# Even layer: input slabs in another order, scan levels among them, the spatial bias on VectorE, output products begun by operand halves

## The reference, cut to what matters

```python
z = h @ w_in
a_u, a_v, b_q, b_f, b_i, b_g = jnp.split(z, [...], axis=-1)      # 512 columns each
a_u, a_v = gelu(a_u), gelu(a_v)
# spatial half: chunks of 128 tokens, 8 heads of 64
v = rms_norm_2(a_v, v_norm)
mixed = einsum('hts,bcshd->bcthd', tril(w_s), v) + b_s.T
a_out = a_u * mixed
# scan half: 4 heads of 128, a gated linear recurrence
f = lb + (1 - lb) * sigmoid(b_f);  k = 1 - f
o_t = q_t . state_t,  state_t = diag(f_t) state_(t-1) + k_t v_t^T   # q = b_q, v = b_i
o = rms_norm_2(o, out_norm) * silu(b_g)
m = concatenate([a_out, o]) @ w_out
```

## Time and profile before

| | |
|---|---|
| median of 3 runs | 1850.38 us (1849.93 to 1851.93) |
| profiled execution | 1851.3 us, its span 1849.3 us |
| TensorE busy | 1744.8 us, 94% |
| VectorE, ScalarE, POOL busy | 1247.6, 878.9, 38.8 us |
| even layer, second input slab to ffn_1 | 912 to 1059 us |

### The profile page before, as it was taken

The page is one execution under the profiler, slowest core; times in us unless marked ns, Lnnn a source line. Parts: engine busy times, 40 slices in busy tenths (PEclk is TensorE's granted clock), DMA queues, the critical chain, the costliest instruction groups (busy, mean ns, idle before and its releaser), DMA issues.

```text
span 1849.3 us, 32552 instructions
## 1 busy us (share of the span) xinstructions
PE 1744.8 (94%) x13634; PEld 1623.0 (88%) x13634; DVE 1247.6 (67%) x1305; ACT 878.9 (48%) x916; POOL 38.8 (2%) x39
## 2 busy tenths in 40 slices
PE   7998997799899999999997899998999999899997
PEld 7987896799899998999995799997999997899997
DVE  5676654774588888666776576667766686576666
ACT  5365332453434436444653454456544462554445
POOL 0000000000000000000003000000000000000000
PEclk9999998899899999999997999998999997899999
DMA  7523334254244453554550245443455441245541
GB/s 282 184 93 114 144 126 156 95 201 161 92 160 190 157 197 137 188 192 166 208 183 36 74 165 202 181 179 140 159 191 194 164 173 51 87 170 192 192 166 63
DMA packets 42646, 286.91 MB, mean 155 GB/s; under 512 B 4704, under 2 KB 6880, under 8 KB 9152
## 3 DMA queue, kind: packets, MB, share of 16 engines
q1 hardware_dynamic: 38528, 273.70, 40.8%
q0 software_dynamic: 2800, 10.69, 1.6%
q10 hardware_dynamic: 1232, 1.25, 0.2%
HBM read 281.42 MB, written 4.19 MB: 154 GB/s over the span
## 4 chain that ended last, share of the span: by engine, by line
PE 84%; DVE 10%; ACT 3%; issue 2%; DMA 1%; POOL 0%; DVEq 0%; ACTq 0%; POOLq 0%
PE PS L367 83%; DVE arena L1664 3%; DVE ring_lo L1661 2%; ACT arena L1132 1%; DVE arena L1661 1%; ACT ring_hi L1132 1%; DMA arena<-in_mem_t 1%; ACT L1132 0%; DVE inv L1718 0%; DMA ring_raw<-in_w_stream 0%; DVE operand L1724 0%; PE PS L706 0%; DVE arena L1797 0%; DVE arena L1792 0%; DVE inv L2383 0%
## 5 line engine op out<-in xcount | busy, mean ns | idle before, releaser
L367 PE MATMUL PS<-operand,ring_hi 128*128 128x256 f32 (+1 forms) x4776 | 1127.2, 321 | 33.2 <-DVE operand L1724 21.5
L367 PEld LDWEIGHTS PS<-operand,ring_hi 128*128 128x128 f32 x4776 | 799.5, 193 | 104.5 <-issue 18.3
L367 PE MATMUL PS<-operand,ring_lo 128*128 128x256 f32 x3092 | 877.2, 284 | 0.0
L1661 DVE TENSOR_TENSOR ring_lo<-ring_raw,ring_hi 128x2048 fp32r<-128x2048 f32 x260 | 599.2, 2308 | 220.0 <-ACT ring_hi L1132 219.7
L1132 ACT ACTIVATE ring_hi<-ring_raw 128x2048 fp32r<-128x2048 f32 x260 | 494.7, 1908 | 226.5 <-PE PS L367 221.4
L367 PEld LDWEIGHTS PS<-operand,ring_lo 128*128 128x128 f32 x3092 | 594.9, 192 | 0.1
L367 PE MATMUL PS<-hidden_hi,ring_hi 128*128 128x256 f32 x880 | 249.0, 283 | 1.3 <-DVE hidden_lo L1661 1.3
L367 PE MATMUL PS<-hidden_lo,ring_hi 128*128 128x256 f32 x880 | 249.0, 283 | 0.0
L367 PE MATMUL PS<-hidden_hi,ring_lo 128*128 128x256 f32 x880 | 248.9, 283 | 0.0
L1132 ACT ACTIVATE arena<-PS 128x512 f32<-128x512 f32 (+4 forms) x123 | 79.7, 660 | 327.2 <-PE PS L367 312.1
L367 PE MATMUL PS<-arena 64*64 64x64 f32 (+7 forms) x2200 | 159.5, 264 | 25.6 <-DVE arena L1664 13.1
(11 more groups left out here) (145 smaller groups left out, 964.5 us busy)
## 6 DMA issues: line engine op xcount, KB each, us to landing
ring_raw<-in_w_stream SPq DMA_DIRECT2D x260, 1024.0 KB, 4.8
spilled_gates<-arena POOLq DMA_DIRECT2D x12, 256.0 KB, 2.3
arena<-spilled_gates POOLq DMA_DIRECT2D x2, 1536.0 KB, 9.3
tables<-in_tables POOLq DMA_DIRECT2D x1, 1344.0 KB, 10.8
residual<-in_x_t ACTq DMA_DIRECT2D x4, 256.0 KB, 6.1
arena<-in_mem_t POOLq DMA_DIRECT2D x1, 1024.0 KB, 13.2
out_t<-residual SPq DMA_DIRECT2D x4, 256.0 KB, 2.1
arena<-in_spatial_t POOLq DMA_DIRECT2D x1, 512.0 KB, 3.7
```

The lines of the kernel that those rows point to most:

```text
L367: return nc.tensor.matmul(out, lhs, rhs, start=start, stop=stop, skip_group_check=True)
L1661: return v.tensor_tensor(out, a, b, op)
```

## The change

The order of the input slabs becomes f, q, v, u, i, g (`EVEN_ORDER`, applied by SP when it issues the DMAs). TensorE does level 0 and 1 of the scan behind the fifth slab and one level behind most slabs after it; spatial mixing stands behind the ninth. Levels 1 to 7 multiply only the later halves of the columns, 64 of 128, into one bank. The bias of spatial mixing leaves TensorE: VectorE multiplies by the gain, now a column of each partition, and adds the bias, which a DMA has laid on 128 partitions, in four fused operations. ScalarE takes exp(-x) of the early and exp(x) of the late half instead of Abs and Exp of everything, takes values v and i out of PSUM itself, and squares v. The first three output slabs run by halves: tiles 0 to 3 of all three, then tiles 4 to 7 of all three, in three banks. The diff, cut to its core:

```diff
+EVEN_ORDER = [4, 5, 2, 3, 8, 9, 0, 1, 10, 11, 6, 7]
...
-        spatial_w = AM = area(14, 8, P)
-        v_gain = area(15, 1, W)
+        spatial_w, AM = area(14, 8, P), area(13.5, 8, HD)
+        spatial_b, v_gain = area(15, 4, P), small[:, 58:62]
+        av_squares, mixed = area(2, 4), area(2, 4)
...
+            stream_turns(3, even // 3 - 1)
+            for n, at in enumerate(EVEN_ORDER):
+                sp.wait_ge(lo_split, even + n - 2)
+                sp.dma_start(ring_raw[:, n % 3, :], stream[even + at]).then_inc(landed[n % 3], 16)
+            turns_ = (N_SLABS - rest) // 3
+            stream_turns(rest, turns_)
...
-            pool.dma_start(spatial_b, ins["spatial_b"]).then_inc(sem("spatial_landed"), 16)
-            pool.dma_start(v_gain[:, 0, :], ins["v_gain"].to_broadcast([P, W])).then_inc(sem("spatial_landed"), 16)
+            for q in range(2):
+                pool.dma_start(spatial_b[rows_of(q)], ins["spatial_b"].rearrange("o (f q s) -> q o f s", f=4, q=2)[q]
+                               .to_broadcast([HD, 4, P])).then_inc(sem("spatial_landed"), 16)
+            pool.dma_start(v_gain, ins["v_gain"].rearrange("o (f p) -> p (o f)", p=P), allow_slow_non_contiguous=True).then_inc(sem("spatial_landed"), 16)
             pool.wait_ge(sem("gl_factors"), 1)
-            pool.wait_ge(sem("spatial_ready"), 1)
             for li in range(1, 9):
...
-            project("even_in", 0, 8, fresh=EVERY, norm=True, by_token=True)
-            project_by_token("even_v", 0, 4)
...
-                        mm(o, AV[:, tt, h * HD:(h + 1) * HD], spatial_w[:, h, :], True, False)
-                        last = mm(o, table("ones")[0:1, 0:HD], spatial_b[:, h * P:(h + 1) * P], False, True)
-            last.then_inc(sem("spatial_mixed"), 1)
...
+            def level(li):
                 pe.wait_ge(sem("gl_factors"), li + 1)
                 if li >= 2:
                     pe.wait_ge(sem("gl_added"), li - 1)
-                if li < 8:
+                if li == 0:
                     for tt in range(2):
-                        tok = slice(tt * P, (tt + 1) * P)
                         for h in range(4):
-                            k = KB[:, h, tok] if li == 0 else XM[li % 2][:, h, tok]
-                            q = BQ[:, h, tok] if li == 0 else XM[li % 2][:, h, tok]
-                            last = mm(bank(2 + 2 * (li % 2) + tt)[:, h * P:(h + 1) * P], k, q)
+                            tok = slice(tt * P, (tt + 1) * P)
+                            last_ = mm(bank(5 + tt)[:, h * P:(h + 1) * P], KB[:, h, tok], BQ[:, h, tok])
+                elif li < 8:
+                    later = halves(XM[li % 2], LEVELS[li - 1])[1]
+                    n = T // (4 * LEVELS[li - 1])
+                    for tt in range(2):
+                        for h in range(4):
+                            o = bank(3 + li % 2)[:, (4 * tt + h) * HD:(4 * tt + h + 1) * HD]
+                            last_ = mm(o.rearrange("p (n c) -> p n c", n=n), XM[li % 2][:, h, tt * P:(tt + 1) * P],
+                                       later[:, h, tt * n:(tt + 1) * n, :])
                 else:
                     for h in range(4):
-                        last = mm(bank(2)[:, h * P:(h + 1) * P], XM[0][:, h, 0:P], XM[0][:, h, P:T])
-                last.then_inc(sem("gl_pairs"), 1)
-            pe.wait_ge(sem("gl_added"), 9)
-            for h in range(4):
-                o, c = bank(6 + h // 2)[:, h % 2 * T:(h % 2 + 1) * T], slice(h * P, (h + 1) * P)
-                mm(o[:, 0:P], BI[:, 0, c], AT[:, h, :])
-                mm(o[:, P:T], BI[:, 1, c], AT[:, 4 + h, :], True, False)
-                last = mm(o[:, P:T], BI[:, 0, c], AC[:, h, :], False, True)
-                if h % 2:
-                    last.then_inc(sem("gl_out"), 1)
-            for h in range(2):
-                pe.wait_ge(sem("gl_squares"), h + 1)
-                mm(bank(2 + h), table("ones"), flat(KB)[:, 512 * h:512 * (h + 1)]).then_inc(sem("gl_norms"), 1)
+                        last_ = mm(bank(3)[:, h * P:(h + 1) * P], XM[0][:, h, 0:P], XM[0][:, h, P:T])
+                last_.then_inc(sem("gl_pairs"), 1)
...
+            def spatial():
+                pe.wait_ge(sem("spatial_ready"), 1)
+                pe.wait_ge(sem("gl_added"), 1)
+                for f in range(4):
+                    for tt in range(2):
+                        for q in range(2):
+                            h = 2 * f + q
+                            last_ = mm(bank(5 + f // 2)[rows_of(q), f % 2 * T + tt * P:f % 2 * T + (tt + 1) * P],
+                                       AV[:, tt, h * HD:(h + 1) * HD], spatial_w[:, h, :])
+                last_.then_inc(sem("spatial_mixed"), 1)
...
+            def even_out(j, first, last_=None):
+                slot, _, g = place(START["even_out"] + j)
+                pe.wait_ge(lo_split, g + 1)
+                for m in range(2):
+                    for k in range(first, first + KT // 2):
+                        last_ = block_product(bank((7, 3, 4)[j])[:, m * T:(m + 1) * T], slot, m * KT + k,
+                                              XH[:, 8 + k, :], XL[:, 8 + k, :], k == 0 and m == 0, k == KT - 1)
+                return last_
+            by_dve, by_act = sem("even_taken"), sem("even_values")
+            even_slab(0, None, fresh=EVERY)
+            even_slab(1, None, between=lambda: norm_sum(True))
+            even_slab(2, None)
+            even_slab(3, (by_dve, 1))
+            even_slab(4, (by_dve, 2), True)
+            pe.wait_ge(by_dve, 4)
+            level(0)
+            level(1)
+            even_slab(5, (by_dve, 3), True)
+            level(2)
+            even_slab(6, (by_dve, 4))
+            level(3)
+            even_slab(7, (by_act, 1))
+            level(4)
+            even_slab(8, (by_act, 2), True)
+            pe.wait_ge(sem("spatial_landed"), 64)
+            spatial()
+            level(5)
+            even_slab(9, (by_dve, 5), True)
+            level(6)
+            even_slab(10, (by_dve, 6), between=lambda: level(7))
+            level(8)
+            scan_out()
+            even_slab(11, (by_act, 3), between=scan_norms)
             operands(1)
-            residual_project("even_out", 8, (4, 6))
+            for j in range(3):
+                even_out(j, 0)
+            operands(2)
+            for j in range(3):
+                even_out(j, KT // 2).then_inc(multiplied, 1)
+            output_slab(START["even_out"] + 3, 8, bank(5))
...
+            def gl_exp(li):
+                act.wait_ge(sem("gl_diff"), li)
+                early, late = halves(DIF[li % 2], LEVELS[li - 1] if li < 8 else P)
+                run(early, early, ACT.Exp, scale=-1.0)
+                run(late, late, ACT.Exp).then_inc(sem("gl_exp"), 1)
...
-                d = flat(DIF[li % 2])
-                step(run(d, d, ACT.Abs))
-                run(d, d, ACT.Exp, scale=-1.0).then_inc(sem("gl_exp"), 1)
...
+            split_slab(even + 12)
+            values(9, BI[:, :, T:2 * T], ACT.Copy)
+            split_slab(even + 13)
...
+            split_slab(even + 14)
             step(last)
             for h in range(2):
                 run(roots[h], roots[h], ACT.Exp, scale=-0.5).then_inc(sem("gl_root"), 1)
+            even_act(7, BG, ACT.Silu)
...
-            dve.wait_ge(sem("spatial_mixed"), 1)
-            mul(flat(AU), flat(AU), bank(0, 2)).then_inc(sem("mixed_gated"), 1)
...
-                if b >= 32:
-                    for r in range(0, P, 2 * b):
-                        last_ = v.tensor_copy(AT[r:r + b, :, r + b:r + 2 * b], src[r:r + b, :, r + b:r + 2 * b])
-                elif li == 0:
-                    last_ = mul(AT, src, per_head("identity", 8))
+                if li == 0:
+                    last_ = mul(AT, bank(5, 2).rearrange("p (h t) -> p h t", t=P), per_head("identity", 8))
                 else:
-                    step(mul(AM, src, per_head(f"level{b}", 8)))
-                    last_ = tt_(AT, AT, AM, ALU.add)
+                    src = bank(3 + li % 2).rearrange("p (h n c) -> p h n c", h=8, c=b)
+                    if b >= 16:
+                        for i in range(HD // b):
+                            r = 2 * b * i
+                            last_ = v.tensor_copy(AT[r:r + b, :, r + b:r + 2 * b], src[r:r + b, :, i, :])
+                    else:
+                        am = AM.rearrange("p h (n c) -> p h n c", c=b)
+                        step(mul(am, src, halves(per_head(f"level{b}", 8), b)[1]))
+                        at = halves(AT, b)[1]
+                        last_ = tt_(at, at, am, ALU.add)
...
+            even_take(3, BQ[:, 2:4])
+            dve.wait_ge(sem("even_taken"), 4)
+            gl_factor(1)
+            split_slab(even + 6)
+            gl_factor(2)
+            gl_mask(0)
+            split_slab(even + 7)
+            gl_mask(1)
+            gl_factor(3)
+            gl_mask(2)
+            dve.wait_ge(sem("av_squared"), 1)
```

(29 more changed lines are left out.)

233 lines of the change are left out of this document (131 added, 102 removed).

## The result

The changed kernel took **1809.99 us** (median of 4 runs, 1809.19 to 1810.89), the kernel before 1850.26 us beside it (1849.93 to 1851.93). The ratio is 0.9785, with a 95% interval of 0.9772 to 0.9798: 40.3 us less. The forecast was 1813 us, with a range of 1806 to 1826.

The account below looks back on a forecast made before the run. TensorE, busy for 94% of the span, was taken as the bound. Terms of 49.7 us plus 0.3, 1.7 and 0.7 made 52.4 in place of 89.9, so 1850.4 - 37.5 = 1813 us, range 1806 to 1826.

Parts of the forecast that it names:

- Spatial mixing: TensorE's 16 products without bias products in the even layer: 3.8 us in place of 17.7, at 0.236 us each.
- Levels 1 to 7: Scan levels on TensorE with half the columns: weights set the pace, 13.3 us; lower bound 7.2 if columns did.
- changes of kind: Nine switches between slab and small products on TensorE that interleaving adds: 0.2 us each, 1.8 us in all.
- Tail wait: TensorE's wait before the scan half of the output operands: 1.7 us in place of 5.48.
- Clock behind it: Half clock on TensorE after the tail's wait: zero to 1.5 us, taken as 0.7.
- First wait: TensorE's wait for the scan's factor 1, after level 0: 0.3 us, upper end 3.
- level 0: First scan level on TensorE, unchanged by the change: 2.05 us.
- level 8 with the scan's output: Last scan level on TensorE, 1.0 us, and the scan output's 12 products, 3.1 us.
- norms: Two norm products of 512 columns on TensorE behind the scan: 1.6 us.
- VectorE and POOL the bound: Rival, chance 0.11: VectorE and POOL become the bound, waits at levels grow by 8 to 15 us, about 1825 us.
- Levels late: Rival, chance 0.07: levels not ready behind their slabs, the scan stays open, only 17.7 us gained, 1833 us.
- Clock down: Rival, chance 0.06: TensorE's clock stays down among slabs; mild form 1823 us (0.04), slower kernel 1869 us (0.02).

Follow-up runs that it names:

- d1: Changed kernel with the spatial mixing products writing output partitions 0 to 63 first, then the eight writing 64 to 127: 1815.87 us, ratio 0.9818.
- a3: Changed kernel with one more product, 64 columns streamed, before each of the 56 products of levels 1 to 7: 1823.08 us, ratio 0.9852.
- a4: Changed kernel with one more product, 128 columns streamed, before each of the 56 products of levels 1 to 7: 1821.97 us, ratio 0.9848.
- a2: Changed kernel with the spatial mixing loops in the old order, both token tiles of one head, then the next head: 1810.86 us, ratio 0.9780.
- d2: Changed kernel with VectorE's mask product of levels 1 to 4 done three times: 1810.51 us, ratio 0.9783.
- c1: Changed kernel with POOL's difference of levels 1 to 7 done twice: 1817.18 us, ratio 0.9830.
- b4: Kernel before with bias on VectorE, output slabs by halves and half columns, slabs and levels in the old order: 1832.49 us, ratio 0.9904.
- b3: Kernel before with only half columns in levels 1 to 7 and two half exponentials, nothing interleaved: 1851.27 us, ratio 1.0014.
- c4: Changed kernel with root exponentials ahead of slab 14's split and second operand halves multiplied in two steps: 1809.62 us, ratio 0.9785.

## Why the prediction held, step by step

The cause was right: slabs as cover for the scan, the clock at 1.00, two short waits. The even layer took 48.3 us in place of the 52.4 of the sum (41.6 us gained, not 37.5). By terms:

- **Spatial mixing, 3.8 us forecast, 2.0 measured**: the step that was mis-sized. The twelve products of the earlier trace rows from which I took 0.236 us all write one half of the output partitions; those of the changed kernel alternate. d1 shows 0.21 us in one half against 0.126 us alternating. Reading the form of a row (64 columns, 128 streamed) was not enough.
- **Levels 1 to 7, 13.3 us, and changes of kind, 1.8 us; measured 12.4 us together** (seven times 1.77). The pace by weights is right (a3, a4: 0.224 us, not 0.238); a change between slab and small products costs nothing that a turn of 7.53 us shows (5.76 + 1.77).
- **Tail wait, 1.7 us; measured 2.72.** I took VectorE's 3.5 us from a kernel that waited for the first operand half only; both halves need 4.37 us. The table loads were priced right by the row: 1.28 us at 993.11 us, and the exponentials begin at 994.40. The Trainium skill, page ScalarE: Activation LUTs, section What ACT_TABLE_LOAD costs, adds a drain of 1.38 us to a load. By it the two loads of the tail would have made the measured wait 5.5 us (an estimate from that page); this trace shows no drain.
- **Clock behind it, 0.7 us; measured 0.** The same wait of 2.72 us is followed by full clock here and in a2, by half clock worth some 1.3 to 1.5 us in a3, a4, d1, d2 and c1. Zero to 1.5 was the right bracket, and no trace says what decides. That the profile of the changed kernel has none of it is luck: it came in five of the seven executions with this wait, and D's 41.6 us would be some 1.5 less with it.
- **First wait, 0.3 us; measured 0.43**, and c1 shows that it is the tight place: a second difference of 1.9 us cost 7.6 us from there on.
- The rest: level 0 1.95 for 2.05, level 8 with the scan's output 3.96 for 4.1, norms 1.88 for 1.6 (half of the 3.59 us of the earlier trace rows would have been 1.8).

These differences sum to -4.0 us; measured -4.1. The terms listed above the forecast sum to 9.7 us, so the upper end of its own range should have read 1823 and not 1821; nothing hangs on it.

Rivals. *VectorE and POOL the bound* (0.11): false, and not near. VectorE was busy for 69.7 us and POOL for 15.1 from 912 to 1000 us; d2's 5.5 us more came through as 0.6, c1's double POOL not at all behind the first turn. That the two hold each other up is real all the same; a ring_lo subtraction (2.28 us alone) takes up to 4.03 us in this timeline of DVE:

```profile
930.51 4.03 DVE L1785 TENSOR_TENSOR ring_lo<-ring_raw,ring_hi 128x2048 fp32r<-128x2048 f32 x1
```

*Levels late* (0.07): none but level 1. *Clock down* (0.06): it was up; b4 shows the same scan without slabs at 0.50.

What I had not seen: part of the turn of the levels in a row was POOL's difference, which held up VectorE's add beside it, so that half the elements shortened the turn by 0.5 us only; and the turn shorter by that much gained nothing, because the clock fell (b3).

## What to carry to other kernels

A chain of short dependent steps is best hidden between long independent work; here that, with the moves that go with it, gave 22 of 42 us, and the clock stayed up, while with shorter steps in a row it fell (b3). Before pricing a product by a row of the same form, look at where the row's neighbours write. When a wait is closed, look for the transfer or split that was released by the end of what you reorder: it is late next (c4).

## What the runs showed of the hardware

- Float32 products with 64 weight columns: 0.126 us each when they write alternating halves of the output partitions, 0.21 when they write one half (d1). With 128 weight columns: 0.224 us for 64 and for 128 streamed columns (a3, a4). All at a granted clock of 1.00.
- An SBUF add on VectorE took 1.96 us over 512 elements beside a POOL subtraction of 1.96, and 1.95 us over 1024; where POOL was idle, two-input operations took 0.69 and 1.22 us (940.64 and 970.91 us in the changed kernel). So POOL's instruction set the time. The Trainium skill, page SBUF — State Buffer, section Who interferes with whom, has this exclusion for whole instructions; the traces agree (the 4.03 us above are 1.75 more than 2.28, and POOL's instruction beside it took 1.89).
- A level that TensorE did in 1.89 us between slabs took 3.67 us among levels alone, at a granted clock of 0.50 (1.2 GHz), although the engine was then busy for 3.67 of every 4 us (b4). In before, with gaps of up to 2.45 us, the grant was 0.66 to 1.00 from 992 to 1016 us. I can't say from these runs what decides it.
